# Two-layer diffusion backbone on one core: turnovers without GpSimd additions, modulation dealt out evenly in the feed-forward and unevenly over the attention branches, projections of the last branch reordered

## The reference, cut to what matters

```python
mod  = silu(c or c_ctx) @ w_mod[l] + b_mod[l]        # 6 x 1024 values, for latent and for context
u    = rmsnorm(h, g_pre_mix) * (1 + scale) + shift
p    = u @ w_in                                      # projections of branches A, B, C, D, and gates
o_b  = softmax(q k^T * s (+ bias)) v                 # A latent attention, B window, C neighbourhood, D dense
y    = sum_b(sigmoid(gate_b) * (o_b @ w_branch[b])) @ w_out
h    = h + gate_mix * rmsnorm(y, g_post_mix)
u    = rmsnorm(h, g_pre_ffn) * (1 + scale2) + shift2
y    = (silu(a) * b) @ w_ffn_out,  a, b = split(u @ w_ffn_in)
h    = h + gate_ffn * rmsnorm(y, g_post_ffn)
```

## Time and profile before

| | |
|---|---|
| median of 3 runs | 2110.29 us (2108.03 to 2114.64) |
| time of the profiled execution | 2106.48 us |
| its span in the trace | 2104.5 us |
| PE, DVE, ACT, POOL busy | 1865.4, 1234.4, 868.8, 865.7 us |
| mean granted PE clock | 0.941 |

### The profile page before, as it was taken

The page is one execution under the profiler, slowest core; times in us unless marked ns, Lnnn a source line. Parts: engine busy times, 40 slices in busy tenths (PEclk is TensorE's granted clock), DMA queues, the critical chain, the costliest instruction groups (busy, mean ns, idle before and its releaser), DMA issues.

```text
span 2104.5 us, 31907 instructions
## 1 busy us (share of the span) xinstructions
PE 1865.4 (89%) x10675; PEld 1601.3 (76%) x10675; DVE 1234.4 (59%) x2277; ACT 868.8 (41%) x1890; POOL 865.7 (41%) x775
## 2 busy tenths in 40 slices
PE   8788899999988899878888799958999998979997
PEld 7566677877777777766766688847788878879997
DVE  6346666666556645477866634356564445676654
ACT  2344444444433443331221123336655544545553
POOL 6333443445444443674453322353425544262101
PEclk9889899999999999888988899969999999989998
DMA  7122233333332223224455533212343433345663
GB/s 277 52 56 58 77 89 97 94 88 107 88 86 66 71 56 120 75 81 125 142 172 163 159 115 95 83 26 62 81 113 100 111 95 91 101 126 156 181 184 122
DMA packets 381804, 223.16 MB, mean 106 GB/s; under 512 B 51606, under 2 KB 377548, under 8 KB 380620
## 3 DMA queue, kind: packets, MB, share of 16 engines
q1 hardware_dynamic: 379340, 217.97, 36.6%
q10 hardware_dynamic: 2304, 3.15, 0.5%
HBM read 217.92 MB, written 3.15 MB: 105 GB/s over the span
## 4 chain that ended last, share of the span: by engine, by line
PE 62%; DVE 13%; issue 10%; DMA 6%; ACT 4%; POOL 4%; DVEq 0%; ACTq 0%; SPq 0%; POOLq 0%
PE bank L1764 18%; PE bank L1765 17%; PE bank L1766 17%; DVE tab L1515 5%; DMA Y<-in_w_mod 4%; PE bank L1983 2%; PE bank L1962 2%; PE bank L1904 1%; PE bank L1832 1%; DMA tab<-in_rpb_c 1%; DVE mod_sums L1515 1%; DVE Z L1659 1%; DVE small L1686 1%; POOL stat L1195 1%; POOL Y L1256 1%
## 5 line engine op out<-in xcount | busy, mean ns | idle before, releaser
L1764 PE MATMUL bank<-Uhi,w_ring 128*128 128x512 f32 (+2 forms) x1664 | 603.4, 363 | 27.5 <-DVE Ulo L1624 18.8
L1765 PE MATMUL bank<-Ulo,w_ring 128*128 128x512 f32 (+2 forms) x1664 | 587.3, 353 | 0.0
L1766 PE MATMUL bank<-Uhi,w_ring 128*128 128x512 f32 (+2 forms) x1664 | 586.7, 353 | 0.0
L1268 POOL TENSOR_TENSOR w_ring<-load_ring,w_ring 128x512 fp32r<-128x512 f32 (+3 forms) x288 | 358.8, 1253 | 272.3 <-issue 147.9
L1308 ACT ACTIVATE w_ring<-load_ring 128x512 fp32r<-128x512 f32 (+4 forms) x640 | 368.9, 602 | 91.6 <-PE bank L1766 72.1
L1764 PEld LDWEIGHTS bank<-Uhi,w_ring 128*128 128x128 f32 (+1 forms) x1664 | 325.8, 196 | 75.2 <-issue 23.8
L1495 DVE TENSOR_TENSOR w_ring<-load_ring,w_ring 128x512 fp32r<-128x512 f32 (+1 forms) x352 | 274.7, 802 | 164.6 <-ACT w_ring L1308 153.5
L1766 PEld LDWEIGHTS bank<-Uhi,w_ring 128*128 128x128 f32 (+1 forms) x1664 | 324.7, 195 | 42.7
L1765 PEld LDWEIGHTS bank<-Ulo,w_ring 128*128 128x128 f32 (+1 forms) x1664 | 325.9, 196 | 36.4
L1764 PE MATMUL bank<-Z,w_ring 128*128 128x512 f32 (+2 forms) x784 | 274.6, 350 | 11.8 <-DVE Z L1659 6.1
L1765 PE MATMUL bank<-Z,w_ring 128*128 128x512 f32 (+2 forms) x784 | 270.9, 346 | 0.0
(11 more groups left out here) (139 smaller groups left out, 2492.5 us busy)
## 6 DMA issues: line engine op xcount, KB each, us to landing
load_ring<-in_w_in SPq DMA_DIRECT2D x192, 256.0 KB, 2.9
load_ring<-in_w_ffn_in SPq DMA_DIRECT2D x160, 256.0 KB, 3.3
Y<-in_w_mod SPq DMA_DIRECT2D x96, 256.0 KB, 2.8
load_ring<-in_w_ffn_out SPq DMA_DIRECT2D x80, 256.0 KB, 3.0
mod_place<-in_w_mod SPq DMA_DIRECT2D x64, 256.0 KB, 2.8
load_ring<-in_w_branch SPq DMA_DIRECT2D x64, 256.0 KB, 2.9
mod_w<-in_w_mod SPq DMA_DIRECT2D x8, 1024.0 KB, 13.7
load_ring<-in_w_in SPq DMA_DIRECT2D x64, 128.0 KB, 2.5
```

Of the source, the lines that this page charges most:

```text
L1268: pool.tensor_tensor(w_ring[:, slot, 1, 0:sz], load_ring[:, plan.slot['load', key], 0:sz], w_ring[:, slot, 0, 0:sz].bitcast(F32), ALU.subt ...
L1764: pe.matmul(dst, lhs[0], rhs[0], start=start, stop=False)
L1765: pe.matmul(dst, lhs[0], rhs[1], start=False, stop=False)
L1766: return pe.matmul(dst, lhs[1], rhs[0], start=False, stop=stop)
```

## The change

It does six things. (1) The feed-forward pieces of layer 0 have their lo half made by DVE, not POOL. (2) Layer 1's modulation gets a budget of 1.2 per weight piece (`point`) instead of 3.7 per tile; it runs on through the output tiles of the feed-forward, up to the last but one; its ring has four places, its sums two places used in turn, and PE's part of a group comes two pieces after DVE's last. (3) Layer 0's modulation is dealt out at 0.2, 0.8, 1.6 and 0.9 steps a slot in branches A, B, C, D. (4) In the turnover, POOL neither adds to H nor makes the full value of U: DVE does all eight `post` steps, reading the broadcast from its bank, and ACT makes the full value and then rounds it to `Uhi`. (5) The sums of y squared end first (`first_sums`), the other two (`sums_rest`) after, in another bank; the second widening and broadcast stand ahead of all `post` steps. (6) Branch D's first unit has its q chain earlier, its v store last.

```diff
-MOD_RATE = 0.92
-MOD_RATE_FFN = 3.7
-POST_POOL = (2, 5, 7)
+MOD_RATE = (0.2, 0.8, 1.6, 0.9)
+MOD_COST = {'modw': (0, 0.96, 1.93), 'modsum': (0, 0.3, 0.3)}
+MOD_US = 1.2
...
+    def point(self, us):
+        self.owed += us
+        self.late = [(key, left - 1) for key, left in self.late]
+        while self.late and self.late[0][1] <= 0:
+            key = self.late.pop(0)[0]
+            self.add_up(key, 2 if key[1] < 16 else 1)
+        while self.todo and self.todo[0][1][0] == self.layer:
+            kind, key, j = self.todo[0]
+            sides = 2 if key[1] < 16 else 1
+            if self.owed < MOD_COST[kind][sides]:
+                break
+            self.todo.pop(0)
+            self.owed -= MOD_COST[kind][sides]
+            if kind == 'modw':
+                self.weigh(key, j, sides)
+            else:
+                self.late.append((key, 2))
...
         p.step('sums', nmo, n=n, what=('ysq', 'hz', 'zsq'))
-        p.step('mstat', nmo, nh=1, dim=D, n=n, after=('sums_done', nmo))
+        p.step('sums_rest', nmo, n=n, what=('hz', 'zsq'))
+        p.step('mstat', nmo, nh=1, dim=D, n=n, after=('first_sums', nmo))
         p.step('wide', nmo, n=n, of=1)
-        p.take('bc', ('bc', nmo), ('bc_copied', nmo))
+        p.take('bc', ('bc', nmo), ('post_scaled', (nmo, KT - 1)))
         p.step('bcast', nmo, n=n)
-        p.step('bccopy', nmo, n=n)
         p.step('moment', nm, n=n)
         p.step('pow', nm, n=n)
-        post(nmo, 0, n)
-        post(nmo, 2, n)
         p.step('wide', nm, n=n, of=4)
         p.take('bc', ('bc', nm), ('ap_scaled', (nm, KT - 1)))
         p.step('bcast', nm, n=n)
-        later = {0: (1,), 1: (3, 5), 2: (4,), 3: (6, 7)}
-        apply(nm, l, which, n, first, {i: [(lambda kt=kt: post(nmo, kt, n)) for kt in kts] for i, kts in later.items()})
+        post(nmo, 0, n)
+        post(nmo, 1, n)
+        apply(nm, l, which, n, first, {kt: [lambda kt=kt: post(nmo, kt + 2, n)] for kt in range(KT - 2)})
...
-            return ks[:3] + qs[:2] + [ks[3], qs[2], ks[4], vs[0], vs[1], ks[5], vs[2], qs[3], ks[6], qs[4], vs[3], qs[5],
-                                      vs[4], qs[6]]
+            return [k0, k1, k_raw, q0, k_sum, q1, q_raw, k_norm, v0, q_sum, k_rot, v1, v_raw, q_norm, k_store, v_turn,
+                    q_rot, q_store, v_store]
...
-                mods.some(MOD_RATE)
+                mods.some(MOD_RATE[min(k // per, 3)])
...
-        if what not in ('gate', 'up', 'y', 'fa', 'fb', 'first') or what in ('gate', 'fa', 'fb') and key[0][1][0] == 0 \
+        if what not in ('gate', 'up', 'y', 'fa', 'fb', 'first') or what == 'gate' and key[0][1][0] == 0 \
...
-                        ins = act.activation(U[0][:, kt, r], tmp[:, plan.slot['tmp', k2], r], ACT.Identity,
+                        ins = act.activation(u[:, r], tmp[:, plan.slot['tmp', k2], r], ACT.Identity,
                                              bias=shift(f['l'], f['which'], kt, side),
                                              scale=is_ab(f['l'], 2 * f['which'])[:, kt, side:side + 1])
-                    ins.then_inc(sem['ap_hi'], 1)
+                    ins.then_inc(sem['ap_full'], 1)
+                    act.wait_ge(sem['ap_full'], count['ap_full', key])
+                    act.activation(U[0][:, kt, 0:f['n']], u[:, 0:f['n']], ACT.Copy).then_inc(sem['ap_hi'], 1)
```

More of the change, by code:

```diff
@@ L716, in output @@
                 key = (nmo, dt)
-                S.extend(p.gemm(('y', key), pieces_of(dt), src, kts, P, nq,
-                                [('y_ready', key), ('ysq_done', key)], need if dt == 0 else {}))
+                for st in p.gemm(('y', key), pieces_of(dt), src, kts, P, nq,
+                                 [('y_ready', key), ('ysq_done', key)], need if dt == 0 else {}):
+                    S.append(st)
+                    if which == 1 and not ends:
+                        mods.point(MOD_US)
+                if dt == KT - 2 and which == 1 and not ends:
+                    mods.rest(l + 1)
+                    for g in range(3):
+                        p.step('coef', (l + 1, g))
                 p.step('yev', key, n=nq, l=l, which=which)
@@ L749, in hidden, with pieces @@
             p.step('fh', k, n=nq)
+        def pieces(made):
+            for st in made:
+                S.append(st)
+                if not last:
+                    mods.point(MOD_US)
         for f in range(2, FT):
             k = (l, f)
-            S.extend(p.gemm(('fa', k), [dict(w='w_ffn_in', l=l, row=4 * j, nk=4, cols=P, starts=[f * P])
-                                        for j in range(2)], 'U', lambda j: range(4 * j, 4 * j + 4), P, nq,
-                            [('ffn_silu', k)]))
+            pieces(p.gemm(('fa', k), [dict(w='w_ffn_in', l=l, row=4 * j, nk=4, cols=P, starts=[f * P]) for j in range(2)],
+                          'U', lambda j: range(4 * j, 4 * j + 4), P, nq, [('ffn_silu', k)]))
             if f == 2:
@@ L760, in build_plan @@
             sigmoid(k)
[L761 to L764 removed]
+            pieces(p.gemm(('fb', k), [dict(w='w_ffn_in', l=l, row=4 * j, nk=4, cols=P, starts=[DFF + f * P])
+                                      for j in range(2)],
+                          'U', lambda j: range(4 * j, 4 * j + 4), P, nq, [('ffn_h', k)]))
             hidden(k)
[L766 to L770 removed]
         nmf = (l, 'post_ffn')
@@ L1126, in _ @@
                     (l, ch), j = key
[L1127 removed]
+                    for name, k_ in plan.freed['mod1' if l else 'mod', key]:
                         sp.wait_ge(sem[name], count[name, k_])
```

209 lines of the change are left out of this document (91 added, 118 removed).

## The result

The changed kernel takes 1995.6 us (median of 4 runs, 1993.6 to 1998.9) where the kernel before takes 2111.2 (median of 4): a ratio of 0.9454, with a 95% interval of 0.9432 to 0.9475. The forecast was 2014 us in a range of 1995 to 2046. Its sum was 96 us less for the profiled execution; between the two profiled executions it is 109.0 us (2106.5 to 1997.5), between their spans 108.9 (2104.5 to 1995.6).

A forecast was written before the change was run, and what follows sets the result against it. Bound: layer 0's feed-forward chain of transfer, weighing and sum, with matmuls waiting; the turnovers next. Terms 75 + 15 + 4 + 2 = 96 us less, from a 2110.3 median to 2014; range 1995 to 2046.

The forecast's parts named there:

- Feed-forward and output tiles: Layer 0's two stages: dense they take 352.6 us against 433.3; 80.7 less 6 of remaining waits gives 75 us less.
- the price that "decides this": A weighing in layer 0's feed-forward: median 0.485 us taken; at the 0.742 average DVE has 228 us for 228.
- Turnovers: The three turnovers and the end: 6 us for the second, 5.5 first, 3 third, 0.5 end; sum 15, bounds 5 and 21.
- (a): Second turnover: the second widening stands ahead of the `post`, 3.2 us less.
- (b): Second turnover: with POOL idle the second widening takes 0.43 us, 1.05 us less.
- (c): Second turnover: first power made while PE ends the other two sums; with hand-overs about 1.4 us less.
- Attention: Attention branches: 4 us less from dealing the modulation (A 8 less, C 3 more, D 1 more), 2 from branch D's order.
- the last branch's order: Branch D's first unit, q chain earlier: at most one 2 to 3 us wait per layer goes, 2 us less.
- R1: Layer 0's feed-forward: DVE becomes the bound, the gain shrinks by about 30 us, time 2044; chance 0.15.
- R4: Feed-forward and output tiles: every weighing waits for its transfer, time 2186; chance 0.03.
- R2: Branch C is overfilled: attention loses 10 us instead of gaining 4, time 2028; chance 0.08.
- R3: The dealing does nothing because something else spaces the pieces; only turnovers and attention gain, time 2089; chance 0.04.

The follow-up runs named there:

- own_bank: The changed kernel with layer 1's modulation sums in a bank of their own, not in the output tiles' ring of three: 1992.6 us.
- pool_splits: The changed kernel with layer 0's feed-forward pieces split by POOL again: 1997.7 us.
- ring_of_two: The changed kernel with two places for layer 1's modulation weights in place of four: 1995.8 us.
- posts_first: The changed kernel with the first two `post` steps ahead of the second widening again in each turnover: 2000.3 us.
- even_rate: The changed kernel with layer 0's modulation dealt at 0.92 per step in all four attention branches: 2000.5 us.
- lumped: The changed kernel with layer 1's modulation dealt 3.7 operations twice a tile, all in the hidden tiles; splits on DVE and four places stay: 1998.1 us.
- sum_at_once: The changed kernel with PE's modulation sum right behind the last weighing, not two points later: 2022.0 us.
- lumped_pool: The changed kernel with modulation dealt 3.7 operations twice a tile in the hidden tiles and the feed-forward splits back on POOL: 2034.6 us.

## Why the prediction was right, and where it was not

**The number was right by little.** The whole gave 109 us where 96 were forecast, and the median lies 0.6 us above the lower end of a range whose lowest sum was called "not all at once". What carried it out so far is attention, which gave more than twice its forecast.

**Feed-forward and output tiles: 75 forecast, 75.6 measured.** The ceiling and the size hold. Of the mechanism one premise does not: the sum did not "follow at once" before, it stood two pieces behind the last weighing as it does now. What was late was DVE, with up to sixteen weighings in a row, two places and weighings of 742 ns. The late sum is what even dealing needs, not what the kernel before lacked. The hidden tiles lie at the low end of 228 to 245 us; the waits of up to 6 us that were kept turned up in the output tiles, 129.1 us against 123 to 128. I had taken them for a late queue; they are a bank that is not yet free, shown by `own_bank`. That the reserve fitted is luck.

**But the price that "decides this" did not decide it.** The step said that DVE would be the bound if a weighing kept its mean of 0.742, because DVE would have 228 us for 228. In `pool_splits` a weighing takes 0.77 on average ((65.2 + 57.8)/160) and nothing is lost. The step had an inner fault: it charged DVE with slow weighings and with the splits, but weighings are slow only while a POOL instruction runs beside them. In `pool_splits` 56 of the 160 take 1381 ns on average, each of them across a POOL instruction, and the other 104 take 482. The Trainium skill, "SBUF — State Buffer", section "Who interferes with whom", which the forecast weighed, says that a DVE instruction with two SBUF inputs contends with a GpSimd instruction that reads SBUF. The trace agrees, by these 1381 and 482 ns. By that rule alone one would have expected the splits' move to matter here, which it does only with lumps (33.2 and 36.4 us against 0.0).

**What the sum of busy times could not see.** The stage is dense at 169 us of DVE work, and has 15 us more with the sum two points earlier at 171 us. Not the share of DVE decides, but whether DVE is through with the last weighing when PE comes to the sum. Added places and fast weighings help it with lumps. Even dealing spares it both, one at a time, but only with the sum two pieces later. The parts are not additive: the splits' move is worth 36 us, 33 or 0, the added places 27 or 1, depending on the rest.

**Turnovers: 15 forecast, 17.9 measured** (7.6, 7.4, 2.1 and 0.9 at the end). Here is the second one, PE and then two rows of DVE, to be read beside the earlier trace rows:

```profile
1262.06 3.00 PE L1882 MATMUL bank<-C,norm_sum 128*128 128x1 f32 x24
1270.04 2.05 PE L1923 MATMUL bank<-C,wide 128*128 128x128 f32 x8
1272.86 2.05 PE L1923 MATMUL bank<-C,wide 128*128 128x128 f32 x8 [0.77 <-DVE wide L1591]
1280.17 0.76 PE L1778 MATMUL bank<-Uhi,w_ring 128*128 128x512 f32 x1 [5.26 <-DVE Ulo L1638]
```
```profile
1268.09 0.43 DVE L1591 COPY wide<-stat 128x512 f32<-128x512 f32 x1 [1.13 <-POOL stat L1234]
1272.29 0.43 DVE L1591 COPY wide<-stat 128x512 f32<-128x512 f32 x1 [1.12 <-POOL stat L1239]
```

From the first sum to the second broadcast it is 10.8 us, where it was 14.7 and the forecast had 9.0; to the first projection 18.1, where 16 to 18 were forecast and 22.4 stood before. The 1.8 us that are missing are the clock, not the plan. PE's same rows in `ring_of_two`, which has the same order there:

```profile
1266.47 2.73 PE L1882 MATMUL bank<-C,norm_sum 128*128 128x1 f32 x24
1272.61 2.05 PE L1923 MATMUL bank<-C,wide 128*128 128x128 f32 x8
1275.43 2.04 PE L1923 MATMUL bank<-C,wide 128*128 128x128 f32 x8 [0.77 <-DVE wide L1591]
1282.73 0.77 PE L1778 MATMUL bank<-Uhi,w_ring 128*128 128x512 f32 x1 [5.26 <-DVE Ulo L1638]
```

The kernel before took 2.73 us for its 24 first sums as well, the changed kernel's trace 3.00, at a granted clock of 0.69 up to the first widening against 0.94 here. Like with like, the second broadcast comes 9.0 us after the first sum and the first projection 16.3 us after it. So (a), (b) and (c) together gave the 5.7 us of the forecast. Item (b) held: both widenings take 0.43. Item (c) held in its effect: the first widening starts 5.0 us after the first sum in place of 7.5. PE's two other sums still stand ahead of the first broadcast and of the moments, and at the lower clock they cost the 1.8 us. Of item (a)'s 3.2 us, by `posts_first`, about 2 reach the projections. What the eight tiles behind gave (36.7 us in place of 39.8) made up for it; I had charged DVE's pace there as a loss.

**Attention: 6 forecast, 15.3 measured.** This is the wrong part. The measured figure is the 14.1 of layer 0's branches and the 1.3 of all other stretches. The dealing was put at 4: it gives 8.5 over the four branches of layer 0, 4.8 in the whole. A moved step was taken as a third of its time in branch A; 14 steps of 1.94 us took 14.6 us away, half of it. C pays 7.2 us for 12 to 13 steps, 0.6 each, where 3 us were charged for all. **The step that failed is the last branch's order, "at most one wait of 2 to 3 us in each layer": it is worth 12.4 us.** Layer 1, with 3.0, was read rightly. In layer 0 the same two norms share DVE with the weighings, and with more of them in branch C two waits of 5 us each were waiting there. The kernel before has such waits in the same place (560 to 650), and I should have looked for them there and asked what the dealing, changed at the same time, would do to them:

```profile
PE bank L1904 <- DVE wide L1570: 6.3, 2, 3.7
```

The two edits seem to work together: in branch C the order is worth 10.4 us at the new rate. At the old rate only the kernel before and `even_rate` can be set side by side, which differ by 6.1 us there, in more than the order.

The rivals: R1 and R4 did not come. R2 was half there: C is overfilled, by 7 us, and the new order hides it. R3 is refuted by the dense stage.

## What to carry to other kernels

An engine that helps out on the side (here the sum that PE makes of DVE's work) should be asked late: with work dealt evenly, two pieces of slack in the order were worth 23 us in two stages at no cost. Look at the order that the list really gives before saying what stands behind what, and at what a budget holds when a stage begins: a left-over one put two bursts of sixteen at the start of this one. Edits that shorten the same chain must be priced together and not one by one; whichever comes first takes the gain. Where a burst of side work is dealt into slots, look at the short instruction behind the burst on which another engine waits, rather than at the share of busy time.

## What the runs showed that I had not expected

- A split on DVE (128x512, two inputs in SBUF) took 860 ns on average in the changed kernel's hidden tiles and 702 in `lumped`, with POOL idle for over 200 us in both. It is the slowing by POOL all the same. POOL still makes one subtraction of 1.29 us for each hidden tile. In the changed kernel 20 of the 79 splits lie across one of them and take 1381 ns on average, the other 59 take 684. In `lumped` two splits meet it, and 17 weighings do instead, at 1489 ns. One such pair, POOL and then DVE:

```profile
951.43 1.30 POOL L1300 TENSOR_TENSOR Z<-fil,Z 128x512 fp32r<-128x512 f32 x1 [10.42 <-ACT Z L1460]
951.89 1.38 DVE L1508 TENSOR_TENSOR w_ring<-load_ring,w_ring 128x512 fp32r<-128x512 f32 x1 [1.28 <-ACT w_ring L1323]
```
- Of PE's idle time at a late sum, the rows show only a part as a wait: in `sum_at_once` 9.6 us at line 1846, with 13.5 us of PEld idle ahead of the sum's weights put down to "issue". The stage is 15.1 us longer. The two rows overlap, and the stage's length is the safer measure.
- Stages that no edit touches differ between traces by the granted clock. In the first turnover, from the first sum to the first projection, it is 17.7 us at 0.58 in the changed kernel and 15.5 us at 0.68 in `even_rate`; `lumped_pool` has 15.5 us too. Branch B of layer 0 takes 162.4 us in `ring_of_two` and 156.2 in the changed kernel, with 8.1 and 8.7 us of waits of PE in all, at 0.95 and 1.00:

```profile
273.40:435.80 162.40, 154.30 (x826) 126.29 (x825) 102.88 (x234) 74.08 (x183) 65.94 (x58) 0.95 0.32 87
273.90:430.10 156.20, 147.45 (x826) 120.83 (x825) 102.56 (x233) 73.92 (x183) 65.92 (x58) 1.00 0.34 91
```

So of one trace each, differences of 2 us in a turnover and of 3 to 6 us in a branch of the attention say nothing before the granted clock of both has been compared. In branch C of `own_bank` and of the changed kernel it is the same, and the 3.5 us between them stay open.
